# A sixth resident expert place, made from gate, norm and modulation memory that is idle early in each expert stage

## The reference, cut to what matters

```
for layer i in 0, 1:
    sh_a, sc_a, g_a, sh_f, sc_f, g_f = split(silu(cond) @ w_ada[i] + b_ada[i], 6)   # one set for each condition
    h   = layernorm(x) * (1 + sc_a) + sh_a
    out = diff_attention(h)                 if i == 0      (8 heads, two softmax maps each)
          fourier_mix(h) @ w_fourier_out    if i == 1
    x   = layernorm(alpha * x + g_a * out) * ln_gain[i, 0] + ln_bias[i, 0]
    h   = layernorm(x) * (1 + sc_f) + sh_f
    moe = top-1 of 4 groups, then top-2 of its 8 experts; each expert is (silu(h @ Wg) * (h @ Wu)) @ Wd
    x   = layernorm(alpha * x + g_f * moe) * ln_gain[i, 1] + ln_bias[i, 1]
```

## Time and profile before

| what | value |
|---|---|
| median of 3 runs | 976.3 us (974.66 to 978.91) |
| span of the profiled execution | 968.9 us |
| own time of the profiled execution | not given apart; the median is 7.4 us over its span |
| instructions | 12777 |
| PE busy | 821.1 us (85%) |
| DVE / ACT / POOL busy | 339.3 / 147.5 / 176.8 us |
| moved by DMA | 321.39 MB, mean 332 GB/s |

### The profile page before, as it was taken

One profiled execution on the slowest core, in us unless ns is written; L12 is line 12 of the kernel. 1 busy time (PEld: TensorE's weight loads), 2 busy tenths in 40 slices (PEclk: granted clock), 3 DMA queues, 4 the chain that ended last, 5 costly groups with the idle time before them and its releaser, 6 DMA issues. The chain is left out here.

```text
span 968.9 us, 12777 instructions
## 1 busy us (share of the span) xinstructions
PE 821.1 (85%) x4895; PEld 419.4 (43%) x4895; DVE 339.3 (35%) x818; ACT 147.5 (15%) x339; POOL 176.8 (18%) x250
## 2 busy tenths in 40 slices
PE   3899999998898897998869788999599987777783
PEld 2555666665457433333323234546433333333331
DVE  3113554556587211111111137848611111101036
ACT  1122222223200111111101012001111110101013
POOL 2041212123122211122111100223212211111100
PEclk9999999999997999999999999999699999999998
DMA  9998493439339897999999979976899999999971
GB/s 333 365 371 305 140 386 112 167 135 342 145 105 387 353 412 290 420 420 418 419 418 419 418 304 356 381 264 230 353 387 418 417 419 418 419 419 420 419 297 65
DMA packets 91020, 321.39 MB, mean 332 GB/s; under 512 B 12686, under 2 KB 25710, under 8 KB 66872
## 3 DMA queue, kind: packets, MB, share of 16 engines
q1 hardware_dynamic: 74400, 289.41, 75.7%
q0 software_dynamic: 12704, 21.86, 6.3%
q10 hardware_dynamic: 3832, 8.99, 2.5%
HBM read 313.62 MB, written 28.90 MB: 354 GB/s over the span
## 5 line engine op out<-in xcount | busy, mean ns | idle before, releaser
L1067 PE MATMUL psum<-ring,arena 128*64 128x512 f32 x880 | 255.2, 629 | 39.1 <-DMA ring<-in_w_expert_up 28.4
L1067 PEld LDWEIGHTS psum<-ring,arena 128*64 128x64 f32 x880 | 84.8, 145 | 169.4 <-issue 166.0
L1089 PE MATMUL psum<-ring,arena 128*64 128x512 f32 x440 | 124.1, 598 | 20.2 <-DVE arena L1883 19.6
L1879 DVE TENSOR_TENSOR arena<-arena,psum 128x256 f32<-128x256 f32 x34 | 14.3, 421 | 283.6 <-ACT arena L1408 277.0
L1067 PE MATMUL psum<-h_hT,arena 128*64 128x512 f32 x208 | 93.1, 601 | 6.0 <-DMA ring<-in_w_expert_up 5.1
L937 PE MATMUL psum<-ring,h_hT 128*128 128x384 f32 x288 | 96.5, 488 | 0.0
L883 PE MATMUL psum<-ring,h_hT 128*128 128x512 f32 x160 | 69.3, 593 | 1.8 <-ACT h_hT L1489 1.5
L684 POOL DMA_INDIRECT y_scratch<-arena,sidx x32 | 33.6, 1048 | 203.9 <-DVE arena L1889 203.9
L937 PEld LDWEIGHTS psum<-ring,h_hT 128*128 128x128 f32 x288 | 53.6, 191 | 34.1
L1089 PEld LDWEIGHTS psum<-ring,arena 128*64 128x64 f32 x440 | 35.6, 136 | 71.2 <-issue 46.8
L1889 DVE COPY arena<-psum 128x512 f32<-128x512 f32 x32 | 22.1, 692 | 120.6 <-PE psum L1089 120.6
(11 more groups left out here) (230 smaller groups left out, 890.0 us busy)
## 6 DMA issues: line engine op xcount, KB each, us to landing
ring<-in_w_expert_down SPq DMA_DIRECT2D x52, 1024.0 KB, 20.6
ring<-in_w_expert_gate SPq DMA_DIRECT2D x50, 1024.0 KB, 19.0
ring<-in_w_expert_up SPq DMA_DIRECT2D x50, 1024.0 KB, 22.2
ring<-in_w_ada SPq DMA_DIRECT2D x24, 2048.0 KB, 15.0
h_hT<-in_w_expert_gate SPq DMA_DIRECT2D x12, 1024.0 KB, 20.4
h_hT<-in_w_expert_up SPq DMA_DIRECT2D x12, 1024.0 KB, 24.0
h_hT<-in_w_expert_down SPq DMA_DIRECT2D x12, 1024.0 KB, 26.5
ring<-in_w_qkv SPq DMA_DIRECT2D x9, 1024.0 KB, 12.5
```

The lines of the kernel that those rows point to most:

```text
L1067: last = pe.matmul(bank[b][64 * e:64 * e + 64, :].rearrange("p (g n) -> p g n", g=2), mem.GT[b][:, c, 64 * e:64 * e + 64], w, start=(c == ...
L1089: last = pe.matmul(bank[5 + half][64 * e:64 * e + 64, :], mem.actT[b][:, f, 64 * e:64 * e + 64], w[:, f, 512 * half:512 * half + 512], sta ...
L1879: V.tensor_tensor(mem.act[b], mem.sil[b], bank[b][:, FE:2 * FE], ALU.mult).then_inc(S["act"], 1)
```

## The change

- `SLOTS` is 6. Places 0 to 3 are the ring, place 4 (`ROW_SLOT`) is `last_slot`, and place 5 (`VECTOR_SLOT`) is new: its gate and up weights lie in `arena` where `gates` and `gb` are, its down weights in a widened `lnscale` tensor.
- Place 5 is used for experts 5, 11, 17 and 23 only (`AFTER`): from pair 12 on there are five places, and the `g_f` rows and the last norm's rows are loaded into their memory: POOL spreads the rows at pair 11, ACT loads the norm's rows at pair 12.
- `m` holds one layer's modulation. Layer 1's bias is loaded by SP during attention, behind `ada(1,1)`, once layer 0's units are stored; `ada_add(1, 0)` waits for it.
- `ada(1,3)` and `ada(1,10)` are loaded into the work area (`U0`) instead of the ring. Expert 1 is loaded earlier in both layers.
- The order of SP's loads changes accordingly; several semaphores are merged; `store_m(0, ...)` comes earlier.

```diff
-SLOTS = 5
+SLOTS = 6
-SLOT_OF = [e % SLOTS for e in range(EXPERTS)]
-SPARE = SLOT_OF[EXPERTS - 5]
+ROW_SLOT, VECTOR_SLOT = 4, 5
+VECTOR_PAIRS = 12
+SLOT_OF = list(range(SLOTS))
+AFTER = {}
+for _e in range(2 * PAIRS):
+    if SLOT_OF[_e] == VECTOR_SLOT and _e + SLOTS >= 2 * VECTOR_PAIRS:
+        continue
+    if len(SLOT_OF) < EXPERTS:
+        AFTER.setdefault(_e // 2, []).append(len(SLOT_OF))
+        SLOT_OF.append(SLOT_OF[_e])
...
-        self.m = sb("m", [P, 2, ADA_UNITS, P])
+        self.m = sb("m", [P, ADA_UNITS, P])
-        self.lnscale = sb("lnscale", [P, D])
+        self.spare = sb("lnscale", [P, 2 * D + 512])
+        self.lnscale = self.spare[:, 2 * D - 512:]
...
+            def load_vector_slot(l):
+                sp.wait_ge(gb_used, 2 * l + 1)
+                load_gate_up(l, VECTOR_SLOT)
+                sp.wait_ge(norm_ready, 6 * l + 6)
+                load_down(l, VECTOR_SLOT)
...
             sp.wait_ge(qkv_ps, 24)
             load("ada", 1, 1)
-            for u in (2, 3):
-                after_ada(1, u - 2)
-                load("ada", 1, u)
+            sp.wait_ge(m_out, 32)
+            for i in range(2):
+                sp.dma_start(mem.m[i:i + 97:32, :, :],
+                             A["b_ada"][1].rearrange("(u j n) -> j u n", u=ADA_UNITS, j=4)).then_inc(bias_in, 16)
+            after_ada(1, 0)
+            load("ada", 1, 2)
+            after_ada(1, 1)
+            load_expert(0, 1)
+            sp.wait_ge(pv_ps, STEPS)
+            for b in range(2):
+                sp.wait_ge(kv_stored[b], 64)
+            load("ada", 1, 3)
             sp.wait_ge(proj_ps, 6)
             for u in (4, 5):
                 load("ada", 1, u)
-            after_ada(1, 3)
-            load_expert(0, 1)
+            load_vector_slot(0)
             after_ada(1, 5)
...
-                    coming = [e for e in (2 * n + SLOTS, 2 * n + 1 + SLOTS) if e < EXPERTS]
+                    coming = AFTER.get(n, [])
...
-                        for t in range(TILES):
-                            sp.wait_ge(y_in[t], 16)
-                        for u in (6, 7):
-                            load("ada", 1, u)
                 if l == 0:
                     sp.wait_ge(main[l]["d_ps"], PAIRS)
+                    for t in range(TILES):
+                        sp.wait_ge(y_in[t], 16)
+                    for u in (6, 7):
+                        load("ada", 1, u)
...
                     after_ada(1, 9)
-                    load("ada", 1, 10)
+                    load_gate_up(1, 1, (1,))
+                    load_down(1, 1)
                     after_ada(1, 8)
                     load_expert(1, 2)
+                    sp.wait_ge(four_sb, 4)
+                    load("ada", 1, 10)
                     sp.wait_ge(proj_ps, 12)
                     load_expert(1, 0)
+                    load_gate_up(1, 1, (0,))
                     after_ada(1, 11)
                     load_expert(1, 3)
-                    after_ada(1, 10)
-                    load_expert(1, 1)
+                    load_vector_slot(1)
                     load_last_slot(1)
...
                 pool.sem_inc(rope_done, 1)
+                if u == 3:
+                    store_m(0, 4, ADA_UNITS, ADA_AT[0, 11], landed=False)
...
-                if l == 0:
-                    pool.wait_ge(proj_used, 6)
-                    for i in range(2):
-                        spread(mem.gates[:, i, :], 0, 5, i, gates_in[i])
...
-                    pool.wait_ge(proj_used, 12)
-                    for i in range(2):
-                        spread(mem.gates[:, i, :], 1, 5, i, gates_in[i])
...
+                    if n == VECTOR_PAIRS - 1:
+                        for i in range(2):
+                            spread(mem.gates[:, i, :], l, 5, i, gates_in[i])
...
-                load_norm(2 * l + 1)
...
                 def first(n, b):
+                    if n == VECTOR_PAIRS:
+                        load_norm(2 * l + 1)
                     silu(S, n, b)
...
                 dve.wait_ge(ada_ps, ADA_AT[l, u])
+                if (l, u) == (1, 0):
+                    dve.wait_ge(bias_in, ROUTER_IN + 16 * 2)
```

More of the change, by code:

```diff
@@ L64 @@
 PLACE.update({("out", 0, 0): "A0", ("out", 0, 1): "A1"})
-PLACE.update({("ada", 1, u): place for u, place in enumerate(("A2", "C1", "A2", "C1", "A0", "A1"))})
+PLACE.update({("ada", 1, u): place for u, place in enumerate(("A2", "C1", "A2", "U0", "A0", "A1"))})
 PLACE.update({("ada", 1, 6): "A0", ("ada", 1, 7): "A1", ("ada", 1, 8): "A0", ("out", 1, 0): "B0", ("out", 1, 1): "B1",
-              ("ada", 1, 9): "B2", ("ada", 1, 10): "B2", ("ada", 1, 11): "A2"})
+              ("ada", 1, 9): "B2", ("ada", 1, 10): "U0", ("ada", 1, 11): "A2"})
 LANDED, _sum = {}, {}
@@ L598, in _ @@
             pool.memset(mem.silu[:, :, :], 0.0).then_inc(zeroed, 1)
-            pool.memset(mem.m[:, :, :, :], 0.0).then_inc(zeroed, 1)
+            pool.memset(mem.m[:, :, :], 0.0).then_inc(zeroed, 1)
             pool.memset(mem.G[2], 0.0).then_inc(zeroed, 1)
@@ L617, in head_root, with store_m @@
                 pool.tensor_tensor(mem.rs_y[:, :], mem.rs_v[:, :], mem.power[:, :], ALU.pow).then_inc(root_out, 1)
+            stored = [0]
+            def store_m(l, first, last, ready, landed=True):
+                pool.wait_ge(ada_done, ready)
+                for i in range(2):
+                    pool.dma_start(m_dram[l, i].rearrange("(u j n) -> j u n", j=4, n=P)[:, first:last, :],
+                                   mem.m[i:i + 97:32, first:last, :]).then_inc(m_out, 16)
+                stored[0] += 32
+                if landed:
+                    pool.wait_ge(m_out, stored[0])
             root(range(TILES))
@@ L838, in columns @@
                 for u in range(4):
-                    last = pe.transpose(bank[7][:, P * u:P * u + P], mem.m[:, l, u, :], ident)
+                    last = pe.transpose(bank[7][:, P * u:P * u + P], mem.m[:, u, :], ident)
                 last.then_inc(col_ps, 1)
@@ L845, in columns_in @@
                 for i in range(2):
-                    last = pe.transpose(bank[3][:, P * (2 + i):P * (3 + i)], mem.m[:, 0, 2 * i + part, :], ident)
+                    last = pe.transpose(bank[3][:, P * (2 + i):P * (3 + i)], mem.m[:, 2 * i + part, :], ident)
                 last.then_inc(col_ps, 1)
@@ L1683, in _ @@
             head_norm(STEPS - 1)
-            def row_tmp(l, t):
-                return mem.tmp0 if l == 1 and t == 0 else mem.tmp[:, t, :]
             def gated_half(l, t, half):
                 i = 0 if t == 0 else 1
-                x, tmp = mem.x[:, t, :], row_tmp(l, t)
+                x, tmp = mem.x[:, t, :], mem.tmp[t]
                 n, part = 6 * l + 2 * t + half + 1, slice(512 * half, 512 * half + 512)
```

100 lines of the change are left out of this document (51 added, 49 removed).

## The result

The changed kernel takes 986.25 us (985.08 to 988.45) where the kernel before took 975.48 beside it on the same chip. The ratio is 1.0122, 95% interval 1.0100 to 1.0144. So it is slower by 1.0 to 1.2%, 10 to 12 us; where I count from the changed kernel I take 1.0113. The forecast was 978.9, and its range ended at 984: too low on both counts. (The intervals of the two comparisons together reach from 8 to 14 us.)

A forecast was written before the change was run, and what follows sets the result against it. DMA was taken to bound the expert stages, and chains of DVE, PE and POOL the rest. Terms -7.5 + 5.0 - 7.5 + 5.0 + 7.2 - 1.0 + 2.6 - 1.2 gave +2.6 us: median 978.9, range 968 to 984.

The forecast's parts named there:

- The bias wait: In attention, DVE's add of ada(1,0) waits for layer 1's bias, queued behind ada(1,1): +7.2 us, bounds 0 and 8.5.
- The first rival: In attention, the bias comes in time or the round absorbs it: sum -4.6 us, 971.7 us; chance 0.20.
- `ada(1,3)` beside the first gate rows: In layer 0, the load slows the gate rows, but DVE later waits 1.11 us for PE's projection: 0, bound +1.
- The stream: In each expert stage, the sixth place saves 7.5 us and gate and norm rows cost 5.0: net 2.5 us gained.
- The third rival: In the expert stages, rows cost nothing because PE comes to bound: sum -7.4 us, 968.9 us; chance 0.11.
- Layer 1's norm rows and columns: Before layer 1's routing, they queue behind ada(1,10): +2.6 us, of which 1.2 comes back at the gather.
- The slower rival: Before layer 1's routing, the queue is 10.6 us deep and the gather returns nothing: +5.5 us, 981.8 us; chance 0.19.
- My 7.4 us from span to median: For the whole kernel, the median of the runs lies 7.4 us above the 968.9 us span, carried unchanged.

The follow-up runs named there:

- e16: The changed kernel as it is, run once more beside the others; ratio to the kernel before 1.0105.
- e2: The kernel before with only layer 1's bias loaded late, by SP behind ada(1,1), and DVE's add waiting for it; ratio to the kernel before 1.0087.
- e1: The changed kernel with layer 1's bias loaded by POOL's queue instead of SP's behind ada(1,1); ratio to the kernel before 1.0032.
- e11: The changed kernel with the bias on POOL's queue and ada(1,3) behind the first gate and norm rows; ratio to the kernel before 0.9984.
- e6: The changed kernel without the sixth place's two loads (five places), rows still behind pairs 11 and 12; ratio to the kernel before 1.0233.
- e12: Changed kernel: bias on POOL's queue, ada(1,3) and ada(1,10) behind rows, VECTOR_PAIRS = 15, gate rows behind pair 14's gate_up, slots' gates later; ratio 0.9972.
- e15: e12 with gate rows behind pair 14's scatter again and norm rows asked for behind pair 15's SiLU; ratio to the kernel before 0.9911.
- e10: The changed kernel with unread PE matmuls, 18 ahead of pair 13's gate_up and 6 ahead of pair 14's; ratio to the kernel before 1.0215.
- e13: The changed kernel with unread PE matmuls, 9 ahead of pair 13's gate_up and 3 ahead of pair 14's; ratio to the kernel before 1.0087.

## Why the prediction was wrong

The sign was right and the size was not: +2.6 us forecast, 10 to 12 measured. Between the forecast and the 12.2 us of the two traces (the table without its first line) lie 9.6 us: 2.4 at the bias wait, 1.9 for `ada(1,3)`, 3.5 for PE's clock in layer 0's routing and first pairs, and 1.8 in layer 0's expert stage. By its own steps:

- **The bias wait: right mechanism, priced too low.** +7.2 forecast, at 8.5 at most. The wait was 8.48 us and the half-speed spell behind it 1.1 (about 3 in e16); by the runs, 8 to 9 in all. I put `ada(1,1)`'s landing at the 17.8 us of the earlier trace rows; it took 19.5 in after, and 17.7 in e2, where the wait was 6.97, as I had it. Why it is slower in the changed kernel (19.7 in e1 too) is open. The spell of half clock was not in my sum. The first rival (bias in time, 0.20) is refuted by e1 and e2.
- **`ada(1,3)` beside the first gate rows: the step that failed.** Forecast 0, bound +1, since 1.11 us of slack lay in front of DVE. I took 2.5 us for the row's load instead of 1.3, and set a delay of 1.2 against that slack. The wait grew by 3.05 us, DVE became the last to arrive, and 1.9 us were left, 4.0 in e16. The other 2.3 us of the table's +4.1 are not this load's. They are the clock in the routing, 0.70 granted instead of 0.80 (PE's last router matmuls take 6.88 us and not 5.53), and they are there in e11 too.
- **The stream: right to 0.2 us.** The sixth place saves 7.3 (forecast 7.5), the rows cost 5.0 and 5.2 (5.0), the landing moved by 2.3 and 2.1 (2.5). The third rival (rows free) is refuted by e6.
- **The clock: a term that the sum lacked.** I took every us of the landing as a us of the stage. In layer 1 PE waits 1.2 to 1.5 us ahead of the last product with five places and starts it at full clock (7.5 us in before, e2 and e6). With six it waits 2.9 us or more and starts at half clock, 8.9 to 10.5 us. Only e12 and e15, where that wait is 0.1 and 0.2, have 7.5, and so have e10 and e13 with their filler. That shows the cause; it is worth 1.4 to 3.0 us in layer 1 at this point. In layer 0 before already waits 3.00 us there, and no loss by the sixth place is shown. Then pair 15 follows by 12.8 us in layer 1 and not by 13.9, since before waited 0.91 us for its weights. So at the y rows the two layers are at -0.7 and -2.1, forecast -2.5 each (-2.0 and -2.4 in e16).
- **Layer 1's norm rows and columns: right in the mechanism, the net partly by luck.** +1.4 forecast, +1.5 in the trace. DVE's wait grew by 2.5 us (forecast 2.6). But from the gather to the restart 17.7 us pass instead of 19.9, so 2.2 came back and not 1.2, and a lower clock in the routing ahead of it (0.72 for 0.83) took 0.8. The slower rival (queue 10.6 us deep, +5.5) is not seen there: the gather gave time back.

With the sizes of the first table the sum is 9.6 (bias and clock) + 4.1 (`ada(1,3)` and clock) - 1.4 + 1.2 - 0.7 + 1.5 - 2.1 = 12.2 us of span. The upper bounds of my terms summed to 12.8, which by 976.3 is 989; I cut the range at 984. My 7.4 us from span to median were 1.8 us of fixed addition and a short profiled run; that moves the base and not the +2.6.

Pairs 0 to 2 of layer 0 took 1.2 us more to the restart, and that is the clock as well: 66.9 us at a granted 0.97, where before has 65.7 at 1.00 and e16, the same kernel as after, 64.9 at 1.00. In e11 it is 69.1 at 0.95. Open is what makes the clock of such a stretch differ between runs of one kernel.

## What to carry to other kernels

A small load that an engine will wait for must not stand behind a large one in the same queue: put it on another queue, even at the same moment. A load moved to a quiet place is not free there: look for the small rows that land at that place, and hold the large load until they are in. Rows that are wanted late belong behind the store that others wait for, and not ahead of it. And when a bottleneck stream gets shorter, ask how long the engine behind it now idles in front of the last piece: here TensorE came out of waits of 8 to 9 us at half speed each time, and out of waits of about 3 us mostly. Last, before a difference between two traces is put down to an edit, compare the granted clock of the stretch in both.

## What the runs showed of the hardware

- Issuing a load holds SP while many are queued. In after, late in a stage, one takes 2 to 6 us of SP where it takes 0.3 to 0.5 with little queued, and the chain of waits runs through SP (SPq 10% of the span). In the stream I saw nothing lost by it: the DMA engines stayed full. In attention the first piece of the bias, 24 KB, held SP for 4.8 us (5.6 in e2) with `ada(1,1)` and part of expert 0 queued ahead of it.

```profile
495.42 2.12 SPq L457 DMA_DIRECT2D ring<-in_w_expert_gate  x1
497.58 5.94 SPq L457 DMA_DIRECT2D ring<-in_w_expert_up  x1
```

- PE's granted clock behind a wait of some us. In before, behind 3.00 us in layer 0 it was 0.50 from 554.2 to 557.0, behind 1.50 us in layer 1 it was 1.00. Behind the filler and 1.93 or 2.49 us of waiting in e13 it was 1.00, behind 3.31 us in after 0.50. The length of the wait alone doesn't settle it: behind 3.26 us in before the product of pair 12 in layer 1 ran at full clock:

```profile
882.73 0.61 PE L1067 MATMUL psum<-h_hT,arena 128*64 128x512 f32 x1 [3.26 <-DMA ring<-in_w_expert_up]
```
